# Two transformer blocks on one core: attention maps handled two heads at a time, and work regrouped around the norms

## The chip, the cores and the metric

The kernel runs on one core of a Trainium2 chip. The metric is the device time of one execution, in microseconds. The engines are TensorE (PE, with PEld its weight load), VectorE (DVE), ScalarE (ACT), GpSimd (POOL) and SyncE (SP), which issues most transfers.

## The reference, cut to what matters

256 tokens of width 1024 pass through two blocks in float32. Shortened:

```python
h = layer_norm(x)
y = hybrid_mixer(h)       # 4 forgetting heads (64), 4 differential heads (two maps of 32 each),
                          # 4 gated recurrent heads (128) with decays exp(cumsum(log_f))
h = layer_norm(ALPHA * h + y)
h = layer_norm(ALPHA * h + memory_attention(h, mem))    # 4 heads of 256
h = layer_norm(ALPHA * h + grouped_moe(h))              # 16 experts, 2 per token
# second block, layer 0
h = norm(ALPHA_2 * h + even_mixer(h))     # 8 latent heads with top-64 keys, 8 window heads with sinks
h = norm(ALPHA_2 * h + cross_attention(h, mem))         # 4 heads of 128
h = norm(ALPHA_2 * h + dense_swiglu(h))
# second block, layer 1
h = norm(ALPHA_2 * h + odd_mixer(h))      # 16 heads, three branches: compressed, selected, window
h = norm(ALPHA_2 * h + cross_attention(h, mem))
h = norm(ALPHA_2 * h + moe_swiglu(h))                   # 8 experts, 2 per token
# one attention map
p = softmax(q @ k.T * scale + bias_and_mask)            # 256 queries x 256 keys
o = p @ v
```

## The kernel before, in words

Every engine has its own hand-written instruction stream; semaphores order them. The stages follow one another in each stream.

**Units and chunks.** A projection is a list of `units` (lines 515 to 612). For each, PE fills PSUM bank `B[2 + u % 2]` (`emit`, L1017) and ACT copies it out (`save_unit`, L1624). A weight chunk (1 MB, a slot of `ring`) is split into a high half by ACT (`weight_highs`, L1600, instruction at L1607) and a low half by DVE (`weight_lows`, L1959, instruction at L1965); PE makes three products per tile (L997 to L999). There are two slots for high halves, so two chunks can be ready ahead. A chunk freed by PE lets ACT and then DVE prepare the next one but one.

**Output projections.** `add` on PE (L1145) makes four column blocks; DVE adds each to `h` and takes its statistics (L2043, L1954). The high half that follows the last block (`feed`, L1831) and its low half (`lows_through_adds`) stand ahead of the norm. `layer_norm` (L1999) asks ACT for a square root (`root`, L1596), scales `h` in two halves (L2017), and PE transposes each (L1068), ACT saving it to `hT` (L1631).

**Attention.** A map is one head's 256 by 256 softmax. Its steps, map by map: PE `logits` (L1160) into `F[m % 2]`; DVE `score_map` (L2051): add the mask into `S` (L2063), take the maximum (L2070); ACT `exps` (L1673), which also sums; DVE `normalise` (L2078): reciprocal (L2082), a gate (L2084), two scalings (L2086); PE `transpose_probs` (L1176) into `F[2 + m % 2]`; ACT `save_probs` (L1683) to `PT` (L1687); PE `values` (L1187); ACT `save_group` (L1689). PE runs `logits(i)`, `transpose_probs(i - 2)`, `values(i - 3)` in turn (L1211). There are three `S` buffers and two `PT` buffers. Stages: `mix1` (4 forgetting, 8 differential maps), `mem1` (4), `mix2` (8 window, 8 latent), `xa0` (4), `mix3` (32), `xa1` (4). In a two-pass float32 matmul the trace has two records per instruction.

**Recurrent heads.** After all of `mix1` is projected, DVE and ACT turn the forget logits into log decays (L2382 to L2397 and L1841 to L1849); PE, DVE, ACT and POOL then work in 8 levels (`hgrn`, L1219; arguments L2413, exponentials L1855, operands on POOL L933, masks L2428). Three mean squares (`sumsq`, L1654 and L1656) follow.

**Bias tiles.** A relative bias of a head is one flip matmul (L1085) of rows that POOL loads (`hankel_rows`, L920): 16 tiles before `mix2`, 8 more (heads 8 to 15) before `mix3`, whose load POOL issues when norm 6 has been scaled (L923). The compressed logits of `mix3` are one small matmul per head and token half (L1555).

**What the change leaves alone.** The two routed layers (`moe1`, `moe2`) and the steps of the dense layer.

Of the kernel before, what the change touches and what calls it, by code (L numbers as in the profile page):

```python
# [29 lines left out]
P = 128  # L30
T = 256
# [138 lines left out]
def two_block_kernel(nc, I, out):  # L170
    ctx = ExitStack()
    with ctx:
# [23 lines left out]
        NS = 3  # L196
        S, S_r = sb_rounded("S", [P, NS, TT, T])
# [51 lines left out]
        Wlv = r.get(2, 4, T)  # L249
        SM = r.get(3, 512)  # L250
# [46 lines left out]
        olatT = qlatT  # L297
        idx_act = r.get(2, TT, T)
# [13 lines left out]
        vc4 = r.get(2, 64)  # L312
        assert r.at <= 15872 - 16 * BIAS_W, r.at
# [58 lines left out]
        logits_ready, scored, max_ready = sem("logits_ready"), sem("scored"), sem("max_ready")  # L372
# [147 lines left out]
        project("mix1", "T", hT, w, dqT, 772, 1, scale=32.0 ** -0.5)  # L520
        project("mix1", "T", hT, w, dkT, 1028, 1)
        project("mix1", "tok", hT, w, dv, 1284, 1)
        project("mix1", "tok", hT, w, hi, 2564, 2)
        project("mix1", "T", hT, w, hqT, 1540, 2, func=ACT.Silu)
        project("mix1", "T", hT, w, hgT, 3076, 2, func=ACT.Silu)
        unit("forget sums", "cum", (nlogf, FOX_H), cumq, ACT.Copy, -1.0)
        unit("mean squares", "sumsq", (halves, dsq, 1.0 / 64), drs)
# [18 lines left out]
        for i in range(2):  # L546
            for j in range(8 * i, 16):
                unit(f"bias tiles {i}", "flip", (j,), biasT[:, j, :])
# [22 lines left out]
            else:  # L571
# [18 lines left out]
                for par in range(2):  # L590
                    adds.append(("compressed logits", None, par, None))
                for par in range(2):
                    unit("compressed probs", "pctr", (par,), pcT[:, par])
                residual("out3", I["od_w_out_2"][0])
            transposes(f"ln{3 * i + 4} transposed", h, hT, 3 * i + 4)
            project(f"xa{i} queries", "T", hT, I["xa_w_q_2"][i], mqT, 0, 2, scale=128.0 ** -0.5)
            residual(f"xa{i} out", I["xa_w_o_2"][i], 4)
            transposes(f"ln{3 * i + 5} transposed", h, hT, 3 * i + 5)
            if i == 0:
                experts("dense", FF_DENSE // COLS)  # L600
            else:
# [7 lines left out]
        maps, groups, map_span = [], [], {}  # L609

        def attention(stage, items):
# [10 lines left out]
            map_span[stage] = (m0, len(maps), g0, len(groups))  # L622

# [7 lines left out]
        def diff_map(j, c):  # L631
            rows = slice(32 * (2 * (j % 2) + c), 32 * (2 * (j % 2) + c) + 32)
            return dict(qk=[(dqT[rows, j // 2, :], dkT[rows, j // 2, :])], mask=chunkmask,
                        coef=neglam if c else None, v=dv[:, :, 64 * j:64 * j + 64], base=64 * (j % 2))
        diff = [([diff_map(j, c) for j in (2 * a, 2 * a + 1) for c in range(2)], yT[:, 2 + a, :]) for a in range(2)]
# [18 lines left out]
        def nsa_maps(j):  # L654
            g = j // 8
            out = []
            for branch, (k, v) in enumerate(((ksT, vs), (kwT, vw))):
                out.append(dict(qk=[(qcT[half(j), j // 2, :], k[half(j), g, :])], mask=bias_of(j),
                                coef=g3[:, :, 3 * j + 1 + branch], v=v[:, :, 64 * g:64 * g + 64], base=64 * (j % 2),
                                compressed=j if branch == 0 else None))  # L660
            return out
        attention("mix3", [(nsa_maps(2 * a) + nsa_maps(2 * a + 1), yT[:, a, :]) for a in range(8)])
# [206 lines left out]
        def _(pool):  # L869
# [72 lines left out]
            for n in range(4, 6):  # L942
                load_gb(n)
# [13 lines left out]
            load_gb(6)  # L957
            pool.wait_ge(normed_half, 14)
            hankel_rows(list(range(8, 16)), 0)
            for n in range(7, 10):  # L960
# [20 lines left out]
        def _(pe):  # L981
# [12 lines left out]
            def product(bank, x_hi_, x_lo_, w_hi_, w_lo_, start, stop):  # L994

                x1, x2, w1, w2 = (v.bitcast(R32) for v in (x_hi_, x_lo_, w_hi_, w_lo_))
                mm(bank, x1, w1, start=start, stop=False)  # L997
                mm(bank, x1, w2, start=False, stop=False)  # L998
                return mm(bank, x2, w1, start=False, stop=stop)  # L999
# [17 lines left out]
            def emit(u):  # L1017
                stage, kind, args, dest, _, _ = units[u]
                x_hi_, x_lo_ = halves_mem if kind in ("T", "tok") and args[0] is memT else halves_hT
                of = {"mem1 values": "mem1 keys", "mix2b": "mix2"}.get(stage, stage)  # L1020
# [1569 lines left out]
```

## Time and profile before

| | us |
|---|---|
| runs | 2647.33, 2657.49, 2663.75 (median 2657.49) |
| the profiled execution | 2651.68 |
| its span | 2649.9 |
| PE busy | 2356.4 (89%) |
| DVE busy | 1630.2 (62%) |
| ACT busy | 1265.9 (48%) |
| POOL busy | 106.2 (4%) |
| mean granted PE clock | 0.924 |

Times in the views are counted from the span's start. Around the span lie 1.8 us that belong to the measured time. Where the stages lie: start and `mix1` projections to 161 us, gates to 178, `mix1` attention to 229, recurrent levels to 277, `out1` to 322, `mem1` to 402, `moe1` 436 to 696, memory keys and bias tiles to 786, `mix2` to 950, `xa0` to 1003, dense layer 1020 to 1211, `mix3` projections 1239 to 1341, its attention to 1455, `out3`, `xa1` to 1532, `moe2` 1556 to 2632.

### The profile page before, as it was taken

Reading aid. Unit: us, or ns where it says so; the run is one execution under the profiler, and the core shown is the slowest. Engines: PE = TensorE matmul, PEld = TensorE weight load, DVE = VectorE, ACT = ScalarE, POOL = GpSimd, SP = SyncE. Lnnn points to the kernel's source line nnn. Section 1 sums busy time; section 2 is a strip of 40 time slices with the busy share of each in tenths; the row PEclk is TensorE's granted clock in tenths of the full one; section 3 lists DMA queues with packets and bytes.
Section 4 is the critical chain, followed back from the end, with each engine's and each line's share of the span. In section 5 each row is a group of like instructions: output and inputs, shape, how many; then the busy total and the mean of one; then the engine's idle time right before and its main releaser. Section 6 shows DMA issues by size and latency. Waiting matters only on the chain.

```text
span 2649.9 us, 31609 instructions
## 1 busy us (share of the span) xinstructions
PE 2356.4 (89%) x12540; PEld 1846.6 (70%) x12540; DVE 1630.2 (62%) x1835; ACT 1265.9 (48%) x1372; POOL 106.2 (4%) x89
## 2 busy tenths in 40 slices
PE   8977697999889887997889869999999999999995
PEld 7965686333568577996755757777778777878774
DVE  4436453111435656775057668878888888888885
ACT  4343342111233534443225347767676767666662
POOL 3002000000000001221000000000000000000000
PEclk9979897999888898998959879999999999999997
DMA  8430125999643024554600249989999999989892
GB/s 272 153 96 1 64 80 192 417 413 416 228 126 125 17 80 160 182 181 151 147 0 1 80 170 361 343 316 343 336 347 328 340 336 328 357 309 361 314 359 108
DMA packets 285683, 592.17 MB, mean 223 GB/s; under 512 B 12123, under 2 KB 118015, under 8 KB 277248
## 3 DMA queue, kind: packets, MB, share of 16 engines
q1 hardware_dynamic: 280000, 571.54, 60.9%
q0 software_dynamic: 5568, 19.06, 2.3%
q8 instruction: 76, 1.25, 0.2%
q14 instruction: 39, 0.32, 0.0%
HBM read 589.45 MB, written 1.11 MB: 223 GB/s over the span
## 4 chain that ended last, share of the span: by engine, by line
PE 74%; DMA 10%; ACT 6%; DVE 6%; issue 3%; POOL 0%; SPq 0%; DVEq 0%; ACTq 0%
PE psF L997 9%; PE psF L999 9%; PE psF L998 9%; PE psB L997 8%; PE psB L998 8%; PE psB L999 8%; DMA ring<-in_moe_w_gate_dram 4%; DMA ring<-in_w_dram 4%; PE psF L1169 3%; PE psB L1204 3%; PE psF L1331 2%; PE psB L1353 2%; ACT arena_rounded L1753 2%; PE psB L1052 1%; PE psF L1182 1%
## 5 line engine op out<-in xcount | busy, mean ns | idle before, releaser
L2252 DVE TENSOR_TENSOR ring_rounded<-ring,arena_rounded 128x2048 fp32r<-128x2048 f32 x224 | 507.0, 2287 | 29.5 <-ACT arena_rounded L1753 29.2
L1753 ACT ACTIVATE arena_rounded<-ring 128x2048 fp32r<-128x2048 f32 x224 | 429.5, 1919 | 196.2 <-DMA ring<-in_moe_w_up_dram 135.3
L997 PE MATMUL psF<-arena_rounded 128*128 128x512 f32 x896 | 360.4, 402 | 3.4 <-ACT arena_rounded L1775 1.5
L999 PE MATMUL psF<-arena_rounded 128*128 128x512 f32 x896 | 355.6, 397 | 0.0
L998 PE MATMUL psF<-ring_rounded,arena_rounded 128*128 128x512 f32 x896 | 354.6, 396 | 0.0
L1965 DVE TENSOR_TENSOR ring_rounded<-ring,ring_rounded 128x2048 fp32r<-128x2048 f32 (+1 forms) x71 | 153.9, 2171 | 191.4 <-ACT ring_rounded L1607 191.3
L997 PEld LDWEIGHTS psF<-arena_rounded 128*128 128x128 f32 x896 | 170.2, 190 | 44.2 <-issue 4.9
L999 PEld LDWEIGHTS psF<-arena_rounded 128*128 128x128 f32 x896 | 169.6, 189 | 39.7
L998 PEld LDWEIGHTS psF<-ring_rounded,arena_rounded 128*128 128x128 f32 x896 | 169.8, 190 | 37.7
L1607 ACT ACTIVATE ring_rounded<-ring 128x2048 fp32r<-128x2048 f32 (+1 forms) x71 | 128.5, 1812 | 118.0 <-PE psF L999 80.7
L998 PE MATMUL psB<-ring_rounded,PT_rounded 128*128 128x512 f32 x448 | 178.2, 398 | 0.0
L2252 DVE TENSOR_TENSOR ring_rounded<-ring,memT_rounded 128x2048 fp32r<-128x2048 f32 x56 | 128.4, 2292 | 45.8 <-ACT memT_rounded L1753 45.8
L2252 DVE TENSOR_TENSOR ring_rounded<-ring,mv_rounded 128x2048 fp32r<-128x2048 f32 x56 | 128.4, 2292 | 32.8 <-ACT mv_rounded L1753 32.8
L997 PE MATMUL psB<-yT_rounded,ring_rounded 128*128 128x256 f32 x464 | 137.7, 297 | 5.8 <-ACT hT L1631 5.6
L1753 ACT ACTIVATE memT_rounded<-ring 128x2048 fp32r<-128x2048 f32 x56 | 107.4, 1918 | 69.4 <-DMA ring<-in_moe_w_down_dram 69.4
L1331 PE MATMUL psF<-ring,arena 128*64 128x512 f32 x512 | 119.1, 609 | 21.9 <-DMA ring<-in_w_dram 21.0
L998 PE MATMUL psB<-memT_rounded,ring_rounded 128*128 128x256 f32 x464 | 136.3, 294 | 0.0
L999 PE MATMUL psB<-yT_rounded,ring_rounded 128*128 128x256 f32 x464 | 136.1, 293 | 0.0
L1753 ACT ACTIVATE mv_rounded<-ring 128x2048 fp32r<-128x2048 f32 x56 | 107.4, 1918 | 57.4 <-DMA ring<-in_moe_w_down_dram 57.4
L1680 ACT ACTIVATE S<-S,small 128x256 f32<-128x256 f32 x144 | 71.9, 499 | 98.8 <-DVE small L2070 98.8
L997 PE MATMUL psB<-memT_rounded,PT_rounded 128*128 128x512 f32 x224 | 93.3, 416 | 15.1 <-DVE PT_rounded L2257 15.1
L997 PE MATMUL psF<-ring_rounded,hT_rounded 128*128 128x256 f32 x320 | 93.5, 292 | 13.0 <-DVE memT_rounded L1988 10.4
(384 smaller groups left out, 4870.8 us busy)
## 6 DMA issues: line engine op xcount, KB each, us to landing
ring<-in_moe_w_gate_dram SPq DMA_DIRECT2D x112, 1024.0 KB, 5.2
ring<-in_moe_w_up_dram SPq DMA_DIRECT2D x112, 1024.0 KB, 5.1
ring<-in_moe_w_down_dram SPq DMA_DIRECT2D x112, 1024.0 KB, 4.9
ring<-in_w_dram SPq DMA_DIRECT2D x96, 1024.0 KB, 8.9
ring<-in_w_in_dram SPq DMA_DIRECT2D x14, 1024.0 KB, 5.4
ring<-in_ff_w_gate_dram SPq DMA_DIRECT2D x11, 1024.0 KB, 7.3
ring<-in_ff_w_up_dram SPq DMA_DIRECT2D x11, 1024.0 KB, 9.7
ring<-in_ff_w_down_dram SPq DMA_DIRECT2D x11, 1024.0 KB, 5.0
```

The source lines that it names most:

```text
L997: mm(bank, x1, w1, start=start, stop=False)
L998: mm(bank, x1, w2, start=False, stop=False)
L999: return mm(bank, x2, w1, start=False, stop=stop)
L1169: last = mm(bank[:, T * t:T * t + T], q[:, P * t:P * t + P], k, start=(i == 0), stop=(i == n - 1))
L1204: last = mm(bank[base:base + w, 2 * piece:2 * piece + T], mp["v"][:, k, piece:piece + w], PT[:, m % 2, k, :], start=(first and k == 0), st ...
L1331: ins = mm(bank[rows(g), :], xgT[:, kk, rows(g)], ws[g][0][:, k, :], start=first_, stop=last_)
L1353: ins = mm(Y[c][rows(g), :], hiddenT[:, ff, rows(g)], ws[g][0][:, f, cols], start=first_, stop=last_)
L1607: ap_(ring_r[:, hi_slot[c], 0:kt * w].bitcast(R32), ring[:, slot_of[c], 0:kt * w], ACT.Copy)\
L1680: ins = ap_(S[:, s, t], S[:, s, t], ACT.Exp, bias=nmx[:, s, t:t + 1], accum_out=ssum[:, s, t:t + 1])
L1753: ap_(w_hi[slot].bitcast(R32), ring[:, slot], ACT.Copy).then_inc(q["high"], 1)
L1965: V.tensor_tensor(ring_r[:, slot_of[c], 0:kt * w].bitcast(R32), raw, ring_r[:, hi_slot[c], 0:kt * w], ALU.subtract).then_inc(weights_low, 1)
L2252: V.tensor_tensor(ring_r[:, slot].bitcast(R32), ring[:, slot], w_hi[slot], ALU.subtract)\
```

## The change

- Attention works on bundles: two maps where heads are 64 wide, else one. The matmuls of the two maps alternate in `logits` and `values`; the reciprocal, the gate and the sink steps serve both maps at once. Logits use all four `F` banks, transposes `B[2]` and `B[3]`. In `mix1`, `mix2` and `mix3` there are six `S` and four `PT` buffers, in arena memory that is free then. Map order in `mix1` and `mix3` is changed so that neighbours belong to different heads.
- Adding the mask and taking the maximum becomes one DVE instruction per token half, `tensor_tensor_reduce`. Forgetting maps keep the two old steps. Maps without a mask (`mem1`, `xa0`, `xa1`) are no longer copied: the maximum and the exponential read PSUM.
- The gate chain goes inside the first units of `mix1` (after the queries, keys and values of the forgetting heads), with the first two level arguments. The later arguments are made one level earlier. The differential squares are made at level 2, the other squares in two halves, and `out1` does its first four row blocks for two column blocks early.
- Behind `out1`, `out2`, `out3` the last high and low halves are made after the square root and after the transposed inputs. Before the dense layer, the two first chunks' halves are spread around the norm.
- Bias tiles 8 to 15 of the second set are made at norms 4 and 5; their rows are loaded after the attention of `mix2`. Norm 6 is followed by the transposes. The ring starts at slot 3 after the dense layer.
- Compressed logits: a pair of heads shares one matmul over 128 rows, `kcT` being block diagonal: 16 matmuls where there were 32.

Cut to its core:

```diff
-        NS = 3
+        NS = 6
...
+            bundles[stage], m = [], m0
+            while m < len(maps):
+                two = maps[m]["v"].shape[2] == 64
+                bundles[stage].append((m, m + 1) if two else (m,))
+                m += 2 if two else 1
...
-            def logits(m):
-                mp, bank = maps[m], F[m % 2]
-                if m >= 2:
-                    pe.wait_ge(scored, m - 1)
+            def logits(bundle):
+                for m in bundle:
+                    if maps[m]["at"] >= 4:
+                        pe.wait_ge(max_ready if "mask" in maps[m] else exp_ready, m - 3)
...
+                    for i in range(n):
+                        for m in bundle:
+                            mp, bank = maps[m], F[maps[m]["at"] % 4]
...
+                            last = mm(bank[:, T * t:T * t + T], q, k, start=(i == 0), stop=(i == n - 1))
...
+                    for k in range(TT):
+                        for m in bundle:
...
+                            last = mm(B[mp["group"] % 2][mp["base"]:mp["base"] + w, 2 * piece:2 * piece + T],
+                                      mp["v"][:, k, piece:piece + w], pt_of(m)[:, k, :],
...
             def attend(stage):
...
+                    if i < len(todo):
+                        logits(todo[i])
+                    if 0 <= i - 2 < len(todo):
+                        for m in todo[i - 2]:
+                            transpose_probs(m)
+                    if 0 <= i - 3:
+                        values(todo[i - 3])
...
-                    ins = V.tensor_tensor(S[:, s], bank, mp["mask"], ALU.add)
...
-                ins = V.tensor_reduce(nmx[:, s], S[:, s], AX.X, ALU.max, negate=True)
+                        for t in range(TT):
+                            ins = V.tensor_tensor_reduce(out=buf[:, t], in0=bank[:, t], in1=more[:, t], scale=-1.0,
+                                                         scalar=-TAKEN, op0=ALU.add, op1=ALU.min,
+                                                         accum_out=nmx[:, n, t:t + 1])
...
+                do(V.reciprocal(scales, sums_))
+                if mp.get("coef") is not None:
+                    do(V.tensor_tensor(scales, scales, mp["coef"], ALU.mult))
...
# ScalarE, inside the projections
+            forget = span("mix1")[0] + 3
+            for u in range(*span("mix1")):
+                save_one(u)
+                if u == forget:
+                    request()
+                    answer(ap_(lame, lams, ACT.Exp))
+                    request()
+                    step.did(ap_(ffe, ffa, ACT.Exp, scale=-1.0))
+                    step.wait()
+                    request()
+                    step.did(ap_(hkT, bcT, ACT.Exp, scale=-1.0))
+                    step.wait()
+                elif u == forget + 1:
+                    answer(ap_(ffe, ffe, ACT.Ln, bias=1.0))
+                    step.did(ap_(bcT, hkT, ACT.Ln, bias=1.0))
+                    step.wait()
+                elif u == forget + 2:
+                    answer(ap_(hkT, hfT, ACT.Sigmoid, scale=-1.0))
...
# ScalarE, recurrent levels
+            for lv in range(2, len(LEVELS)):
+                level_decay(lv)
+                if lv == 2:
+                    save("differential squares")
             for a in range(2):
-                ins = ap_(oT[:, 2 * a:2 * a + 2, :], pair(B[a]), ACT.Copy)
-            answer(ins)
+                act.wait_ge(hg_pv, 2 * len(LEVELS) + a)
+                answer(ap_(oT[:, 2 * a:2 * a + 2, :], pair(B[a]), ACT.Copy))
             save("mean squares")
             feed("out1")
             root()
+            feed_last("out1")
...
# VectorE, recurrent levels
-                if lv + 1 < len(LEVELS):
-                    level_argument(lv + 1)
+                if 3 <= lv + 2 < len(LEVELS):
+                    level_argument(lv + 2)
...
# TensorE
-            add("out1")
+            add("out1", early=4)
...
+                        for jj in range(8):
+                            last = mm(F[a % 4][:, 32 * jj:32 * jj + 32], qcT[:, jj, P * t:P * t + P], kcT[:, jj // 4, :],
+                                      start=True, stop=True)
...
# GpSimd
+            load_gb(4)
+            pool.wait_ge(o_saved, groups_end("mix2"))
+            hankel_rows(list(range(8, 16)), 0)
+            load_gb(5)
...
-            pool.wait_ge(normed_half, 14)
-            hankel_rows(list(range(8, 16)), 0)
```

## Rows read from the trace of the kernel before

**Rows 1.** Windows: stretch: us, then busy us (instructions) of each engine, granted clock, DMA.

```profile
161.00:178.00 17.00, 2.38 (x14) 2.08 (x12) 6.19 (x9) 12.57 (x13) 0.00 (x0) 0.67 0.19 62
178.00:229.00 51.00, 49.94 (x176) 28.50 (x176) 27.66 (x71) 21.09 (x64) 0.00 (x0) 0.81 0.00 0
229.00:277.00 48.00, 34.86 (x273) 33.34 (x272) 27.56 (x36) 8.84 (x9) 21.24 (x16) 0.89 0.00 1
277.00:298.00 21.00, 7.25 (x21) 3.77 (x19) 6.78 (x9) 12.73 (x14) 0.00 (x0) 0.72 0.00 0
...
865.00:924.00 59.00, 49.02 (x196) 30.26 (x198) 43.07 (x108) 32.50 (x103) 0.00 (x0) 0.86 0.00 1
...
1341.00:1382.00 41.00, 39.37 (x96) 21.37 (x97) 21.16 (x51) 13.80 (x45) 0.00 (x0) 0.50 0.00 0
1382.00:1455.00 73.00, 72.28 (x322) 40.08 (x320) 54.98 (x148) 39.38 (x124) 0.00 (x0) 1.00 0.00 1
1560.00:2649.00 1089.00, 1026.49 (x4488) 821.32 (x4488) 880.67 (x568) 721.56 (x497) 0.00 (x0) 0.97 0.90 321
```

**Rows 2.** Timeline of ACT at the start and in the gate chain.

```profile
68.40 0.20 ACT L1833 ACTIVATE small<-small 128x2 f32<-128x2 f32 x1 [1.52 <-DVE small L2371]
...
163.93 1.28 ACT L1841 ACT_TABLE_LOAD   x1
...
174.33 1.06 ACT L1849 ACTIVATE arena<-arena 128x1024 f32<-128x1024 f32 x1
```

**Rows 3.** Groups of PE, 1383 to 1448 us (`mix3`): xcount | busy us, mean ns.

```profile
L1169 PE MATMUL psF<-arena 64*128 64x256 f32 x88 | 24.8, 402 | 0.0
L1204 PE MATMUL psB<-PT,arena 128*64 128x256 f32 x88 | 23.7, 392 | 0.0
L1182 PE MATMUL psF<-cw,S 128*128 128x128 f32 x91 | 15.0, 286 | 0.0
L1197 PE MATMUL psB<-arena 15*64 15x256 f32 x23 | 7.5, 401 | 0.0
```

**Rows 4.** Groups of DVE, 1383 to 1448 us.

```profile
L2063 DVE TENSOR_TENSOR S<-psF,arena 128x512 f32<-128x512 f32 x23 | 15.9, 691 | 12.3 <-PE psF L1169 12.3
L2070 DVE TENSOR_REDUCE small<-S 128x2 f32<-128x512 f32 x22 | 15.1, 686 | 0.7
L2086 DVE TENSOR_SCALAR S<-S,small 128x256 f32<-128x256 f32 x44 | 13.6, 351 | 0.8
L2084 DVE TENSOR_TENSOR small<-small,g 128x2 f32<-128x2 f32 x22 | 3.6, 161 | 0.8
```

**Rows 5.** Groups of ACT, 1383 to 1448 us.

```profile
L1680 ACT ACTIVATE S<-S,small 128x256 f32<-128x256 f32 x44 | 22.0, 500 | 30.3 <-DVE small L2070 30.3
L1687 ACT ACTIVATE PT<-psF 128x512 f32<-128x512 f32 x22 | 12.6, 574 | 0.0
```

**Rows 6.** Timeline of PE: first logits of two window heads; the `uv` unit.

```profile
865.93 1.14 PE L1169 MATMUL psF<-arena 64*128 64x256 f32 x8 [0.59 <-ACT arena L1642]
...
923.86 2.22 PE L1107 MATMUL psB<-arena,wuv 128*64 128x256 f32 x16 [0.47 <-ACT arena L1694]
```

**Rows 7.** Timeline of DVE: a `tensor_tensor_reduce` and its read-out, `mix2`.

```profile
814.97 0.28 DVE L2464 CUSTOM_DVE_ANT_0 arena<-arena 128x128 f32<-128x128 f32 x1
815.17 0.08 DVE L2464 DVE_READ_ACCUMULATOR2_ANT small<- 128x1 f32 x1
```

**Rows 8.** Timeline of DVE at norm 1.

```profile
324.19 2.29 DVE L1965 TENSOR_TENSOR ring_rounded<-ring,ring_rounded 128x2048 fp32r<-128x2048 f32 x1 [0.59 <-ACT ring_rounded L1607]
326.39 0.38 DVE L2009 BATCH_NORM_AGGREGATE small<-small 128x2 f32<-128x24 f32 x2
```

**Rows 9.** Timeline, norm 6: rows loaded, then the bias tiles.

```profile
1217.27 0.91 POOL L923 DMA_DIRECT2D arena<-bias_rows  x1 [16.70 <-DVE h L2017]
...
1225.84 8.46 PE L1085 MATMUL psB<-arena,cw 128*128 128x384 f32 x16 [15.36 <-issue]
```

**Rows 10.** Timeline of PE: the compressed logits.

```profile
1320.18 13.01 PE L1555 MATMUL psF<-arena 64*128 64x15 f32 x64 [0.40 <-ACT arena L1670]
```

More of the change, by code:

```diff
@@ L546, in two_block_kernel @@
         for i in range(2):
-            for j in range(8 * i, 16):
-                unit(f"bias tiles {i}", "flip", (j,), biasT[:, j, :])
+            if i == 0:
+                for j in range(16):
+                    unit("bias tiles", "flip", (j,), biasT[:, j, :])
             transposes(f"ln{3 * i + 3} transposed", h, hT, 3 * i + 3)
@@ L594, in two_block_kernel @@
                 residual("out3", I["od_w_out_2"][0])
+            if i == 0:
+                for j in range(8, 12):
+                    unit("bias tiles again", "flip", (j,), biasT[:, j, :])
             transposes(f"ln{3 * i + 4} transposed", h, hT, 3 * i + 4)
@@ L597, in two_block_kernel @@
             residual(f"xa{i} out", I["xa_w_o_2"][i], 4)
+            if i == 0:
+                for j in range(12, 16):
+                    unit("last bias tiles", "flip", (j,), biasT[:, j, :])
             transposes(f"ln{3 * i + 5} transposed", h, hT, 3 * i + 5)
@@ L605, in two_block_kernel @@
                 routed("moe2")
-        maps, groups, map_span = [], [], {}
+        more_s = {stage: Region(at).get(3, TT, T) for stage, at in more_at.items()}
+        more_pt = {stage: Region(0 if stage == "mix2" else at + 3 * TT * T).get(2, TT, T) for stage, at in more_at.items()}
+        maps, groups, map_span, bundles = [], [], {}, {}
         def attention(stage, items):
@@ L1019, in emit @@
                 x_hi_, x_lo_ = halves_mem if kind in ("T", "tok") and args[0] is memT else halves_hT
-                of = {"mem1 values": "mem1 keys", "mix2b": "mix2"}.get(stage, stage)
+                of = {"mem1 values": "mem1 keys", "mix1b": "mix1", "mix2b": "mix2"}.get(stage, stage)
                 bank = B[2 + u % 2]
@@ L1568, in _ @@
                 add(f"xa{i} out")
+                if i == 0:
+                    run("last bias tiles")
                 run(f"ln{3 * i + 5} transposed")
@@ L1906, in _ @@
                 feed(f"out{i + 2}")
+                if i == 0:
+                    tiles = span("bias tiles again")[0]
+                    for u in (tiles, tiles + 1):
+                        save_one(u)
                 root()
+                if i == 0:
+                    for u in (tiles + 2, tiles + 3):
+                        save_one(u)
+                feed_last(f"out{i + 2}")
                 save(f"ln{3 * i + 4} transposed")
@@ L1912, in _ @@
                 if i == 0:
-                    for part in range(2):
-                        dense_high(0, 0, part)
+                    tiles = span("last bias tiles")[0]
+                    for u in (tiles, tiles + 1):
+                        save_one(u)
                 root()
+                if i == 0:
+                    for u in (tiles + 2, tiles + 3):
+                        save_one(u)
+                    dense_high(0, 0, 0)
                 save(f"ln{3 * i + 5} transposed")
```

500 lines of the change are left out of this document (278 added, 222 removed).

## The prediction, made before the changed kernel ran

> **What bounds the kernel now.** I read the chain of waits first, then the busy shares in windows by stage, then groups and timelines of the stages that the change touches. The chain shows `moe1` (260 us), the dense steps (190 us) and `moe2` (1076 us) as stretches of their own, whose inner steps stay; the last of them is PE-bound, 1026.49 of 1089 us busy [rows 1]. So the change can move only what lies between. There the windows show four kinds of time:
>
> - gates: 17 us in which PE is busy 2.38 and ACT 12.57 [rows 1]. Each function begins with a table load of 1.28 us, and full-size functions take 1.06 [rows 2];
> - attention: PE is busy throughout, 72.28 of 73 us in the second part of `mix3`, and also 39.37 of 41 us in its first part, but there at a granted clock of 0.50, the lower of its two levels (1.2 against 2.4 GHz). 96 records in 41 us against 322 in 73 us: 0.43 against 0.227 us a record [rows 1];
> - recurrent levels: PE 34.86 of 48 us, POOL 21.24 [rows 1];
> - squares: 21 us with PE 7.25 and ACT 12.73 busy [rows 1].
>
> All sums are against the profiled execution, 2651.7 us (span 2649.9 and 1.8 around it); the median of the runs is 5.8 above it.
>
> **1. Start.** ACT loads a table (1.28), idles 1.52 for DVE and computes 0.20 before it saves the bias rows, and PE waits for that [rows 2]. The change moves this behind: 2.9 us.
>
> **2. Gates, 11 us.** The chain of 17 us goes. What stays behind the last projection is ACT's save (0.6) and high half (1.9), then the cumulative sum: 3 us. So 14 are saved. The chain now lies inside units of 5.8 us each (85 us of `mix1` for 14 chunks). ACT has 2.5 us of work in such a unit, so 3.3 are free, but the order is in line: two loads, two exponentials and a wait for DVE come to 5. The halves for the next but one chunk have only about 1 us to spare, so I expect one stall of 1 us, and 2 more where DVE's scans and level arguments (2.4 and 2.8 us) stand ahead of a low half. Bounds: 0 and 8 us (every piece of the chain uncovered beyond its unit). I take 3, the nearer to the counted slack.
>
> A page bears on it: the Trainium skill, "ScalarE: Activation LUTs", under what ACT_TABLE_LOAD costs, says some 2.7 us, and that one table set holds both ln and exp. The rows show 1.28 us, and the trace has a load at every turn between the two. By the page's price the five loads that are moved would cost 7 us more in place of the 1 us stall; the measured duration decides.
>
> **3. Attention, by pairs.** One map of `mix3` at full clock costs PE four records of each kind: logits 24.8/88 x 4 = 1.13, values 1.08, transposes 0.66, and for every second map 0.65 of compressed values [rows 3]; 2.92 with overlaps. Do two alternating matmuls run side by side? The trace before has both cases. The first two window heads lie on rows 0 to 63 and 64 to 127: their 8 records take 1.14 us, what 4 take in steady state. Two 64-column halves alternate in `uv`: 16 records in 2.22 us, 0.14 each against 0.27 [rows 6, 3]. So a pair costs PE 1.13 + 1.08 + 1.1 (transposes don't pair) + 0.33 = 3.6 us, less overlaps 3.4.
>
> DVE for a pair: the mask step and the maximum, 0.69 each per map [rows 4], become two fused instructions. The trace has them at 128 elements only, 0.28 us with a read-out of 0.08 mostly under the next [rows 7]; with the slope between this and 0.69 at 512 I get 0.42, with read-out 0.45. Bounds at 256 elements: 0.31 (the scaling) and 0.69 (the full-width step), a spread of -0.6 to +1.0 us a pair. Pair: 4 x 0.45 + 4 x 0.31 + two small ops 0.36 with gaps + 0.1 = 3.5 us. ACT: 4 x 0.5 + 2 x 0.57 [rows 5] + 0.2 = 3.3. The three engines are close, so I take a step of 3.65 us, bound by DVE, where two maps took 5.84.
>
> A pair in the low-clock stretch is bound by PE: 3.4 x 1.9 = 6.4.
>
> The Trainium skill, "TensorEngine Tiling (Array Packing)", under the PSUM bottleneck, warns that tiling speeds TensorE and not the evacuation. By PE alone the step would be 3.4; by the warning it is DVE's. The rows agree with the warning, and what more it could cost is the second rival.
>
> *`mix3`*: before 113 us (1341 to 1455). How long the lower clock lasts is open: after an idle stretch it stayed 17 us in `mix2`, 31 from the gates on, 41 here. I take 30: fill 5, four pairs at 6.4, twelve at 3.65, inputs for `out3` 2.5 of 4.5 us, drain 5: 82. With 17 us it would be 74, with 41 us 87. Gain 31 (26 to 39).
> *`mix1`*: before 51, its first 20 us at the low clock because PE had idled for the gates. Now PE comes warm. Forgetting pairs: 4.6 us of logits each (the cumulative part is 128 rows and doesn't pair), then five steps at 3.5 to 4.7 and a drain of 5: 32. Gain 19 (10 if the clock falls all the same).
> *`mix2`*: 59 before. Four window pairs, three of them still slow at 5.8, and eight single maps at 2.75 where they took 3.1 (the fused step; PE then binds): 48. Gain 10.
> *`mem1`, `xa0`, `xa1`*: one copy of 0.69 less ahead of each maximum: 0.7 + 1.7 + 1.7 = 4.
>
> **4. Recurrent levels, 9 us.** Two levels' operands exist at the start (before, PE waited 7 us). Then each level needs 3.85 us of PE, against 4.8 before, since an argument no longer stands behind the masks. Against this stands the differential square at level 2: its two table loads and functions, 12.7/3 = 3.9 us less the copies [rows 1], delay level 3 by 3.8. 48 becomes 38. DVE's share of a level is 3.7 to 3.8 us under POOL's use of memory, so the bound could flip: 4.0 a level, a gain of 8.
>
> **5. Squares and `out1`, 16 us.** From the last level to the end of `out1` it was 45 us. Now two squares of 3.9 follow one another on ACT (8.4 us after the level), then 2.7 of DVE: pair 3 comes at 11. Meanwhile PE makes 48 of the 192 products (6 us). The other 144 take 17, and the third and fourth weight halves are late by 1.3: 11 + 17 + 1 = 29.
>
> **6. Norms 1, 4, 7: 8 us.** Between the statistics and the aggregate stand the high and the low half, 2.29 us and the wait ahead of it; 2.85 us go [rows 8]. They come later, with 5.8 us of cover in the first unit. At norm 4 ACT saves two tiles and a high half ahead of the transposed blocks, 0.5 late. 2.85 + 2.3 + 2.85. The rows of the bias are loaded after `mix2`; before, they needed 8.6 us (1217.27 to 1225.84) [rows 9], and 24 us of `out2` cover that.
>
> **7. Norm 5, 3 us.** The second high and low half (a landing at 1005.2, then 1.9 and 2.3) leave the path: 5 us earlier, but DVE's tail of the norm then meets POOL's low half and holds the first dense step: 3.
>
> **8. Norm 6, 15 us.** PE waited until 1225.84 for the rows and spent 8.46 us on eight tiles [rows 9]. Products began at 1238.7. Without them they start when ACT, after its two high halves (1214.8 to 1218.7), has saved the four transposed pairs: 1223.2.
>
> **9. Compressed logits, 6.5 us.** 64 records of 0.203 us [rows 10], set by the weight load and not by the 15 columns; 32 remain.
>
> Sum: 2.9 + 11 + (31 + 19 + 10 + 4) + 9 + 16 + 8 + 3 + 15 + 6.5 = 135. 2651.7 - 135 = 2516.7; with the median 5.8 above the profiled execution, 2522 us.
>
> **The rivals.**
> *Alternating matmuls don't overlap* in the long run (10 records of mode changes instead): PE stays at 2.92 a map, which gives back 28 us in `mix3`, 7 in `mix1`, 5 in `mix2`: 2562. Against it speak [rows 6]. 5%.
> *Hand-offs bind*: in-order waits between three engines at 90% load make the step 4.5, and the fused instruction is at its upper bound: 26 pairs x 0.85 = 22 us: 2544. For it: the engines are nearly even. 22%.
> *The lower clock stays through attention*, as PE is less busy: 12 pairs of `mix3` at 6.4 in place of 3.65 add 33, `mix1` adds 9: 2564. Against it: in `mix2`, 49.02 of 59 us busy, it rose after 17 us. 7%.
> *Slower than before*: the lower clock also holds in the projections that follow those stages. They hold about 390 us of products at full clock, twice that at the lower. From 135/390 = 35% of them on, the gain is gone; at 45% the time is 2522 + 175 = 2697. Nothing shows the clock low in a dense run of products beyond 17 us. 2%.
> *No effect*, the moved work landing on another queue in full: 2650. 2%.
> *My forecast*: 62%, of which a quarter is a clock that rises early, 2508.
>
> **Range.** The forecast's own terms give 2495 to 2545 (the low clock 17 to 41 us in `mix3`, the fused step's bounds, the stalls in the gates 0 to 8). With the first three rivals: 2488 to 2574.
>
> Faster by over 1%: 0.96; within 1% (about what a measurement of this kernel can tell from no change): 0.02; slower by over 1%: 0.02.
>
> **What would show it.** Logits of a pair as 8 records in 1.15 us; values likewise; in `mix3` at full clock 3.65 us a pair with DVE above 90% busy; no PE gap of 14 us before the cumulative sum, at most 3 us of gaps in `mix1`'s projections; 3.85 us a level from level 4 on; 29 us from the last level to the end of `out1`; first product 8 us after norm 6's square root; compressed logits in 6.5 us. Wrong would be a PE still contiguous in `mix3` at over 5 us a pair, a fused instruction above 0.6 us, or `moe2` longer than 1076 us.

## The result and the profile after

| | before | after |
|---|---|---|
| median | 2652.41 (4 runs) | 2498.85 (4 runs: 2491.49 to 2503.91) |
| profiled execution | 2651.68 | 2497.97 |
| its span | 2649.9 | 2496.2 |
| mean granted clock | 0.924 | 0.947 |

The ratio of the times (after over before) is 0.9424, with a 95% interval of 0.9365 to 0.9483: faster by 154 us. The forecast was 2522 (2488 to 2574). Direction and range held; the gain was 19 us larger than the 135 of the sum.

Windows of the kernel after, by stage. The columns are the stretch and its us, the busy us (instructions) of PE, PEld, DVE, ACT and POOL, the granted clock, then the DMA share and GB/s. They answer to [rows 1]: the wait for the gates, the attention of `mix1`, the recurrent levels, squares with `out1`, the attention of `mix2`, that of `mix3`, and `moe2`.

```profile
163.00:166.00 3.00, 1.28 (x13) 1.19 (x11) 0.04 (x1) 2.46 (x3) 0.00 (x0) 1.00 0.45 152
166.00:199.00 33.00, 27.05 (x176) 17.69 (x176) 23.00 (x79) 22.91 (x67) 4.95 (x4) 1.00 0.05 19
199.00:241.00 42.00, 34.50 (x275) 32.83 (x276) 28.23 (x34) 11.11 (x13) 18.46 (x12) 0.96 0.00 1
241.00:271.00 30.00, 25.57 (x196) 23.73 (x196) 17.44 (x22) 14.93 (x13) 0.00 (x0) 1.00 0.33 106
810.00:855.00 45.00, 36.19 (x196) 25.08 (x194) 31.01 (x128) 30.61 (x101) 0.07 (x1) 0.89 0.00 1
1245.00:1308.00 63.00, 57.51 (x416) 35.48 (x416) 50.13 (x231) 50.55 (x168) 0.00 (x0) 0.96 0.00 1
1406.00:2496.00 1090.00, 1026.05 (x4493) 820.61 (x4491) 882.31 (x569) 722.96 (x498) 0.00 (x0) 0.97 0.90 321
```

The instruction counts of PE are about those of before (416 records in the attention of `mix3`, 418 then); the stages are shorter. How long the clock was low in a window follows from its column: with the two levels 1.00 and 0.50 it is 2 x (1 - clock) x length. For `mix3` that is 63 x 0.08 = 5 us, where [rows 1] have 41 us in one piece. `moe2` has not changed.

Timeline of PE in the same stage, two pairs of maps: start, us, engine, line, operation, tiles, instructions; in brackets the idle time before and what ended it.

```profile
1272.23 1.13 PE L1232 MATMUL psF<-arena 64*128 64x256 f32 x8
1273.29 1.10 PE L1242 MATMUL psB<-cw,S 128*128 128x128 f32 x8
1274.32 1.08 PE L1266 MATMUL psB<-arena 128*64 128x256 f32 x8
1275.34 1.14 PE L1232 MATMUL psF<-arena 64*128 64x256 f32 x8
1276.91 0.63 PE L1242 MATMUL psB<-cw,S 128*128 128x128 f32 x4 [0.43 <-ACT PT L1777]
1277.39 0.63 PE L1242 MATMUL psB<-cw,arena 128*128 128x128 f32 x4
1277.94 0.65 PE L1256 MATMUL psB<-arena 15*64 15x256 f32 x4
1278.52 1.08 PE L1266 MATMUL psB<-PT,arena 128*64 128x256 f32 x8
1279.54 1.13 PE L1232 MATMUL psF<-arena 64*128 64x256 f32 x8
```

Eight records of logits take 1.13 us and eight of values 1.08, what four of each took in [rows 3]. From logits to logits it is 3.11 us for the pair without the compressed branch and 4.20 with it: 3.655 on average, the 3.65 of the prediction. The groups of VectorE from 1256 to 1300 us (xcount | busy us, mean ns) show the fused step:

```profile
L2200 DVE CUSTOM_DVE_ANT_0 S<-psF,arena 128x256 f32<-128x256 f32 x24 | 8.9, 421 | 4.9 <-PE psF L1232 4.9
L2224 DVE TENSOR_SCALAR S<-S,small 128x256 f32<-128x256 f32 x24 | 7.0, 349 | 0.3
L2200 DVE DVE_READ_ACCUMULATOR2_ANT small<- 128x1 f32 x47 | 3.9, 83 | 0.0
```

One lasts 0.42 us, as taken. Its read-out is hidden, though, and the next begins before its end: four in a row start 0.35 us apart, where I had 0.45.

Stage by stage, gains from the timelines of PE in both kernels:

| step | forecast | measured |
|---|---|---|
| 1 start | 2.9 | 0.8 |
| 2 gates | 11 | 11.1 |
| 3 attention of `mix3` | 31 | 50.3 (113.2 to 62.9) |
| `mix1` | 19 | 18.4 (51.1 to 32.6) |
| `mix2` | 10 | 12.8 (57.4 to 44.7) |
| `mem1`, `xa0`, `xa1` | 4 | 5.6 |
| 4 levels | 9 | 6.4 (48.2 to 41.8) |
| 5 squares, `out1` | 16 | 15.0 |
| 6 norms 1, 4, 7 | 8 | 7.3 |
| 7 norm 5 | 3 | 4.2 |
| 8 norm 6 | 15 | 16.2 |
| 9 compressed logits | 6.5 | 6.0 |
| all else | 0 | -0.4 |

The last row hides shifts of up to 2.3 us in both directions in stages whose instructions are the same; a term under 2 us is not to be read more closely. Steps 1 and 5 to 8, some 43 us, are read from the two timelines alone; no run below varies them by themselves.

### The profile page after: what moved, and what is told of

Its sections match the earlier page's. It is cut to its first block, busy times and chain, and to the rows that moved or that the text cites. A ratio compares the mean times of both kernels' runs of the same rounds, so it can differ in the third digit from the quotient of the medians.

```text
span 2496.2 us, 31567 instructions
## 1 busy us (share of the span) xinstructions
PE 2250.2 (90%) x12508; PEld 1791.1 (72%) x12508; DVE 1580.0 (63%) x1887; ACT 1255.6 (50%) x1370; POOL 109.0 (4%) x89
## 4 chain that ended last, share of the span: by engine, by line
PE 71%; DMA 11%; ACT 8%; DVE 7%; issue 2%; SPq 0%; POOL 0%; DVEq 0%; ACTq 0%; POOLq 0%
PE psF L1039 9%; PE psF L1041 9%; PE psF L1040 9%; PE psB L1039 8%; PE psB L1040 8%; PE psB L1041 8%; DMA ring<-in_w_dram 4%; DMA ring<-in_moe_w_gate_dram 4%; PE psF L1399 2%; PE psB L1421 2%; ACT arena_rounded L1848 2%; PE psB L1094 2%; PE psB L1266 1%; ACT ring_rounded L1680 1%; PE psF L1232 1%
## 5 line engine op out<-in xcount | busy, mean ns | idle before, releaser
L1399 PEld LDWEIGHTS psF<-ring,arena 128*64 128x64 f32 x512 | 40.4, 141 | 92.3 <-issue 92.3
L1041 PE MATMUL psB<-mv_rounded,PT_rounded 128*128 128x512 f32 x264 | 104.2, 395 | 0.0
```

Of the source, the lines that this page charges most:

```text
L1041: return mm(bank, x2, w1, start=False, stop=stop, skip_group_check=open_groups)
L1399: ins = mm(bank[rows(g), :], xgT[:, kk, rows(g)], ws[g][0][:, k, :], start=first_, stop=last_)
```

## Experiments

Each starts from the kernel after unless said otherwise. Effects of under 1% are read from stages of the profile.

**Maps of a pair one after the other.** Is it the alternation that makes matmuls overlap?

```diff
-                for piece in range(0, width, P):
-                        for m in bundle:
+                for m in bundle:
+                    for piece in range(0, width, P):
```

and the same in `logits`.

> The changed kernel, but with the two maps of a pair computed one after the other by TensorE (logits and values), all else kept: buffers, fused maximum, order of the stages. Theory (alternating matmuls on the two halves of the array run side by side): a pair of mix3 then needs 2.2 of logits, 2.1 of values, 1.1 of transposes and 0.33 of compressed values, 5.7 us in place of 3.65, so the attention of mix3 grows from 63 us by at least 33, that of mix1 from 33 by about 12, that of mix2 by about 4: some 50 us in all. Rival (the deeper buffers and the shorter VectorE work made the gain, the order of the matmuls nothing): the step stays below 4.2 us and the time within 12 us. On the clock, which stayed low for 6 us of mix3's attention where it had been 41: if the denser pairs bring it back, it is low for 20 us and more here and mix3's attention takes 105 us or more; if the shorter stage ahead of the attention does, it is low for about 6 us again and the attention takes 96 to 99.

Measured: 2515.5 us, ratio 0.9468 (0.9427 to 0.9509). Windows over the attention of `mix1` and of `mix3`:

```profile
164.00:214.00 50.00, 48.10 (x175) 28.36 (x175) 22.84 (x79) 22.60 (x66) 4.94 (x4) 0.60 0.03 11
1260.00:1323.00 63.00, 57.69 (x416) 36.76 (x416) 50.54 (x231) 50.59 (x168) 0.00 (x0) 0.95 0.00 1
```

The logits of a pair in the timeline of PE, in `mix3`:

```profile
1287.66 1.14 PE L1232 MATMUL psF<-arena 64*128 64x256 f32 x8
```

In `mix3` nothing changed: 63.1 us, and the eight records still take 1.14 us, though in the program both matmuls of the one map now stand before those of the other. So my theory was wrong about alternation, and the stated rival did not hold either, as the records do overlap. In `mix1` the stage took 50.8 us. There each map of a forgetting head has full-height matmuls of its cumulative part behind its half-height one, so that taking the maps in turn parts the two halves; and the clock was low for 40 of 50 us. That the one led to the other is argued, not shown. The next run separates the two properties.

**Full-width work between the halves.**

```diff
-                    if i < len(todo):
-                        logits(todo[i])
+                    for p in range(2):
+                        if i < len(todo):
+                            logits(todo[i][p:p + 1])
```

and so for `transpose_probs` and `values`: one map's three steps, then the other's.

> The changed kernel, but TensorE takes the pair map by map: logits, transposes and values of the first map, then those of the second, so that the full-width transposes stand between the matmuls of the two halves of the array. Buffers, VectorE and ScalarE are as in the change. The run before showed that inside a pair the order of the matmuls does not matter. Theory (matmuls of different halves run side by side when nothing of full width stands between them): here they don't, a pair costs TensorE 5.7 us in place of 3.65, mix3's attention goes from 63 to 97 us or more, the whole time up by some 45. Rival (the overlap was never what shortened the stage; deeper buffers and a lighter VectorE were): mix3's attention stays under 68 us. On the clock: if the pairs bring it back, it stays low here for 20 us and more of mix3's attention; if not, for 3 to 9 us as in the four profiles of the change so far.

Measured: 2565.8 us, ratio 0.9679 (0.9644 to 0.9713). The same two windows:

```profile
166.00:225.00 59.00, 57.28 (x176) 31.84 (x176) 23.57 (x79) 23.92 (x69) 4.94 (x4) 0.68 0.04 12
1279.00:1386.00 107.00, 105.39 (x416) 58.88 (x416) 51.36 (x231) 53.06 (x168) 0.00 (x0) 0.85 0.00 1
```

One map of `mix3` in the timeline of PE:

```profile
1329.67 1.13 PE L1234 MATMUL psF<-arena 64*128 64x256 f32 x4
1330.73 0.66 PE L1244 MATMUL psB<-cw,S 128*128 128x128 f32 x4
1331.32 1.08 PE L1270 MATMUL psB<-arena 128*64 128x256 f32 x4
```

Four records need the 1.13 us of eight again; two maps take 3.22 + 2.65 = 5.87 us where they took 3.65. `mix3`'s attention is back at 106.8 us, with 32 us of it at the lower clock. (The profile is of this kernel's slowest execution, 2581.3 us.) With everything else of the change in place, this order alone gives back 67 us (0.9679 - 0.9424 of 2652): the neighbourhood of the two halves carries 44% of the gain (by the two intervals, 67 us give or take some 18), and buffers and fused steps without it shorten `mix3` by only 6 us.

**The kernel before, once more, and with filled gaps.** First unchanged:

> The kernel before, unchanged, for a second profile. If the 40 us of lower clock in mix3's attention and the 19 us in mix1's belong to its instructions, they come again within 7 us; if they are chance, they differ by more, as the 0 and 13.7 us of lower clock did that two profiles of the same instructions of the changed kernel show in mix1's attention.

Then with unread matmuls of 128x128 on 512 columns in its waits:

```diff
+            filler(14)
             pe.wait_ge(logf_ready, 1)
...
+                    filler(4)
                     pe.wait_ge(proj_saved, saved("compress parts"))
...
+                    filler(5)
                     pe.wait_ge(cmp_ready, 1)
```

> The kernel before with such matmuls in its three waits: 14 in the 14 us ahead of the cumulative sum, 4 and 5 ahead of mix3's attention. If the gaps were why the clock was low in the attention stages (19 and 29 us of mix1's, 40 and 40 us of mix3's in two profiles), it is now low for less than 10 us of each, mix1's attention takes 41 to 43 us and mix3's 94 to 98. If the unpaired matmuls themselves keep it low, mix3's attention still has 25 us and more at the lower clock and takes 106 or more.

Windows of the unchanged kernel's second profile (attention of `mix1`, of `mix3`):

```profile
180.00:236.00 56.00, 54.59 (x176) 30.82 (x176) 27.91 (x71) 21.54 (x66) 0.00 (x0) 0.74 0.00 0
1347.00:1460.00 113.00, 111.44 (x416) 61.29 (x416) 75.65 (x199) 52.53 (x167) 0.00 (x0) 0.82 0.00 1
```

Windows with fillers: the filled gap, `mix1`, the end of the fillers ahead of `mix3`, `mix3`:

```profile
164.00:178.00 14.00, 11.56 (x31) 5.64 (x29) 5.90 (x9) 10.27 (x12) 0.00 (x0) 0.94 0.17 58
178.00:233.00 55.00, 53.97 (x176) 30.60 (x176) 27.94 (x71) 21.20 (x65) 0.00 (x0) 0.74 0.00 0
1337.00:1341.00 4.00, 3.27 (x15) 1.73 (x13) 3.96 (x7) 1.08 (x2) 0.00 (x0) 1.00 0.00 0
1341.00:1454.00 113.00, 110.86 (x416) 60.53 (x416) 75.66 (x199) 52.78 (x168) 0.00 (x0) 0.83 0.00 1
```

And `mix3`'s attention with fillers in two parts:

```profile
1341.00:1381.00 40.00, 38.47 (x96) 20.40 (x97) 20.68 (x51) 13.50 (x44) 0.00 (x0) 0.53 0.00 0
1382.00:1454.00 72.00, 71.39 (x318) 39.53 (x316) 54.83 (x148) 39.28 (x124) 0.00 (x0) 1.00 0.00 1
```

The 41 us in `mix3` came again to the microsecond; in `mix1` it was 29 where it had been 19, outside the 7 us that I had allowed. With the gaps filled the clock was at its upper level when `mix3`'s attention began (1.00) and nearly throughout the gap ahead of `mix1` (0.94), and yet 38 us of the one stage and 29 of the other ran at the lower. So the gaps were not the cause: in `mix3` the clock fell 2.6 us after the unpaired attention had begun, and stayed low while PE was busy for 38.47 of 40 us. Being unpaired is not the whole of it either. In all three profiles of these instructions the clock rose with some 73 us of the same unpaired work left, and stayed up to the end (1.00 over the last 72 us here, and over 73 us in [rows 1]). What brings it back, no run shows.

**Sixty-four compressed logits, as before.**

```diff
-                        for jj in range(8):
-                            last = mm(F[a % 4][:, 32 * jj:32 * jj + 32], qcT[:, jj, P * t:P * t + P], kcT[:, jj // 4, :],
+                        for t in range(TT):
+                            for jj in range(8):
+                                last = mm(F[a % 4][:, o:o + N_CMP], qcT[half(j), j // 2, P * t:P * t + P],
```

> The changed kernel with the compressed logits as before: 64 matmuls of 15 columns in place of 32. The stage grows by 6.0 to 6.5 us. On the clock: if the shorter stage ahead of mix3's attention is why the clock came back 6 us into it, it now stays low for 20 us and more of it and mix3's attention grows by another 7 us or more; if the pairs bring it back, the attention stays at 63 to 66 us.

One run, 2510.7 us. The logits took 13.01 us against 7.04, 6.0 more; `mix3`'s attention stayed at 62.8 us (clock 0.97). The shorter stage ahead is not what brought the clock back. `mix1`, whose instructions are those of the change, took 36.7 us, with 14 at the lower clock.

**Gate chain behind the projections.** The blocks of ScalarE and VectorE that ran after units 3 to 5 of `mix1` stand behind `mix1b`.

> The changed kernel with the gate chain behind the last projection of mix1. TensorE idles 13 to 15 us ahead of the cumulative sum again and the two stalls of 0.7 and 1.7 us in the projections go: 11 us more. On the clock: it falls in this gap. If pairs bring it back, it is low for less than 10 us of the attention, which grows from 33 to at most 38; if the clock goes by its own time after a gap, it stays low for most of the attention, as in the kernel before (19 us), and the attention takes 42 or more.

One run, 2515.5 us. From the first transposes to the attention it took 7.7 us more, not 11: PE waited 9.6 us, not 14. (The changed chain lets the cumulative sum go as soon as its own operand is there; that this is the difference is argued, not tried.) The clock fell in the gap and was back 6 us into the attention, then was low for 14 more: 39.5 us in all, between the two expectations.

**Fused step undone.**

```diff
-                        for t in range(TT):
-                            ins = V.tensor_tensor_reduce(...)
+                        do(V.tensor_tensor(buf, bank, more, ALU.add))
+                        ins = V.tensor_reduce(nmx[:, n], buf, AX.X, ALU.max, negate=True)
```

> The changed kernel with the fused addition-and-minimum undone: one full-width addition and one full-width maximum per map. Theory (TensorE sets the 3.65 us step by now and VectorE has 0.5 us of slack): VectorE's work per pair grows from 3.2 by 1.4 to 4.6, so the step becomes 4.6 and mix3's attention grows by about 14 us, mix2's by 4, mix1's by 2: 20 in all. Rival (TensorE's own work covers it): step up to 3.9, under 6 us in all.

Measured: 2528.9 us, ratio 0.9541 (0.9505 to 0.9576); `mix3` 74.7 us, `mix2` 51.3, `mix1` 39.1.

```profile
1259.00:1333.00 74.00, 59.23 (x416) 36.37 (x414) 68.16 (x167) 52.69 (x167) 0.00 (x0) 0.92 0.00 1
```

VectorE is busy 92% now and PE 80%. Steps alternate 3.52 and 4.76 us, 4.14 on average where no halves for `out3` are made; I had expected 4.6. The fused step is worth some 30 us once the halves overlap, again give or take 18; 25 of them lie in `mix1`, `mix2` and `mix3` of the profile.

**Compressed values left out, and four maps of scores.** Which engine sets the step, and do the buffers matter?

```diff
-                    if mp.get("compressed") is not None:
-                        mm(B[g % 2][mp["base"]:mp["base"] + 64, 0:T], vc4[rows, j // 8, :], pcT[rows, j % 2, j // 8, :],
```

> The changed kernel without the compressed branch's values: the 15-row matmuls of every second pair are left out, so the compressed branch is missing from the output. Theory (TensorE sets the step by its own work, 3.55 of 3.65 us): the long step of 4.21 us shortens by 0.65 to about 3.6, the mean to 3.35, mix3's attention from 63 to 58. Rival (VectorE, ScalarE and the hand-offs between the three set it): the mean step stays above 3.55 and the attention above 61.5 us.

```diff
-        NS = 6
+        NS = 4
```

> The changed kernel with room for 4 maps of scores in place of 6. Theory (the depth carries a part of the gain): VectorE may score a pair only when TensorE has transposed the pair before last, which it does after the new logits, so a loop of scoring 1.4, normalising 1.5 and transposing 1.1 us closes at 4.2 us a pair with its waits; mix3's attention goes from 63 to about 72. Rival (the 6 buffers are slack): it stays within 2 us.

Windows over `mix3`'s attention, without the compressed values and with four maps:

```profile
1246.00:1306.00 60.00, 53.10 (x384) 34.05 (x384) 50.10 (x231) 50.35 (x168) 0.00 (x0) 0.95 0.01 1
```

```profile
1253.00:1327.00 74.00, 60.60 (x416) 37.03 (x416) 50.48 (x231) 50.81 (x167) 0.00 (x0) 0.92 0.00 1
```

Without 0.65 us of PE work in every second pair the long step fell from 4.20 to 3.53 or 3.63 us, the average to 3.37, and the attention to 59.8 us. PE's own work set the step, but closely: two later steps, behind VectorE's halves for `out3`, took 3.90 and 3.89 us with waits of 0.71 us for ScalarE, and the stage came out between the 58 of the theory and the 61.5 of the rival. With four maps the steps are 3.71 and 4.87 (4.29; 4.2 expected) and the attention takes 74.4 us: the depth is part of the gain. Each of these two is one run (2497.1 and 2518.1 us) and read by its stage.

**Differential squares later.**

```diff
-                    if lv == 2:
+                    if lv == 5:
                         pe.wait_ge(squares_ready, 1)
...
-                if lv == 2:
-                    save("differential squares")
+            save("differential squares")
...
-                if lv == 4:
+                if lv == 7:
```

Three stalls of PE in the levels of the kernel after led there. Timeline of PE (after):

```profile
204.94 1.16 PE L1295 MATMUL psB<-arena 128*128 128x128 f32 x8 [1.29 <-DVE arena L2581]
...
213.21 1.01 PE L1318 MATMUL psF<-arena 128*128 128x128 f32 x3 [2.68 <-POOL arena L976]
...
223.75 0.94 PE L1295 MATMUL psB<-arena 128*128 128x128 f32 x6 [2.63 <-DVE arena L2581]
```

ScalarE shows the second one's cause, the table load and function ahead of level 3's exponentials:

```profile
207.70 1.28 ACT L1736 ACT_TABLE_LOAD   x1
208.99 0.63 ACT L1736 ACTIVATE arena<-arena 128x512 f32<-128x512 f32 x1
209.53 1.99 ACT L1955 ACTIVATE arena<-arena 128x1024 f32<-128x1024 f32 x2
```

> The changed kernel with the differential squares later: TensorE computes them at level 5, ScalarE takes their two functions behind all levels' exponentials, VectorE their product and halves at level 7. Theory (of the 41.8 us of the recurrent levels, 2.7 are ScalarE's table loads ahead of level 3's exponential and 2.6 VectorE's product and halves ahead of level 4's masks, at a time when all three engines still prepare levels): the first stall goes in full, the second becomes under 1 us, since VectorE idles 1.1 us in each half level at the end; the levels take 37 to 38 us, the time falls by 4. Rival (the levels' own chain over VectorE, ScalarE and GpSimd is late anyway): they stay above 40 us.

Measured: 2493.6 us, ratio 0.9386 (0.9348 to 0.9424). The levels took 35.9 us in place of 41.8, with stalls of 1.29, 0.72 and 0.32 us left. As a time it is not told from the change (the intervals overlap); as a stage it is 6 us.

**Fillers ahead of `mix3`,** with the `filler(4)` and `filler(5)` shown above, and then in every longer wait.

> The changed kernel with matmuls that nobody reads, 128x128 on 512 columns, in two waits of TensorE ahead of mix3's attention: 4 in the 4.2 us after the hidden parts and 5 in the 5.5 us of the compressed softmax. Theory A (idleness of TensorE lets the clock fall there): the 27 us of lower clock from 20 us ahead of the attention on don't come or are shorter than 10; compressed logits and probabilities get 2 to 3 us faster, the attention falls from 63 to 58 or 59. Theory B (it is the thin matmuls, of few rows or columns, that lower it, and full ones alone hold it): the clock comes back by the filler, ahead of the attention, but falls again; 2 to 4 us in all. Rival (the fillers at the lower clock take 1.7 us each and end late): the time rises by 3 to 6 us.

One run, 2499.2 us. The stretch from the hidden parts to the attention took 37.5 us in place of 40.7. Windows from 1224 on: the fillers and small steps, the compressed logits and second fillers, the first pairs:

```profile
1224.00:1234.00 10.00, 8.86 (x73) 5.68 (x68) 0.00 (x0) 7.61 (x11) 0.00 (x0) 0.97 0.81 267
1234.00:1244.00 10.00, 10.00 (x28) 6.54 (x28) 5.40 (x14) 0.60 (x1) 0.00 (x0) 0.51 0.00 0
1244.00:1257.00 13.00, 8.58 (x60) 5.78 (x58) 12.60 (x48) 8.83 (x31) 0.00 (x0) 1.00 0.00 0
```

The clock stays up to 1233, past the first fillers; it falls 1.3 us into the compressed logits and stays low through most of the second fillers, though PE has not a free microsecond in these 10. It went as theory B said (3 us), but which property of the small matmuls counts was not varied.

> The changed kernel with the late differential squares (6 us of the recurrent levels in the run above) and with unread full matmuls in the waits of TensorE at the norms, ahead of the dense step, ahead of mix3's attention and ahead of moe2: 2 to 5 of 0.85 us in waits of 2 to 6 us. If the clock falls at the norms because TensorE waits there, the stretches of lower clock of 7 to 14 us at norms 4 to 8, and the 27 and 10 us ahead of moe2, shrink to less than half in sum; with 3 us of the stage ahead of mix3 that gives 2499 - 6 - 3 - 10 = 2480 us. If the fillers only end late, at 1.7 us each at the lower clock, the time is that of the late squares alone, 2493, or above. Under the ratio 0.9386 of the late squares alone would be a gain by the fillers.

Measured: 2489.2 us, ratio 0.9383 (0.9356 to 0.9410). Against 0.9386 for the late squares alone the fillers bring nothing that can be told, although the mean granted clock rose (0.953 to 0.959 in the five executions, 0.942 to 0.947 with the late squares alone). The first product of `moe2` came at 1407.0 us, 7 us earlier than in the profile of the late squares alone (1414.2), but `moe2` itself took 3 us more; and ahead of the dense layer five fillers took 7.5 us, as they ran at the lower clock themselves. It is the lowest median of the study, but its interval overlaps that of the change.

## Why the prediction was right, and where its sizes were off

**The part on which the sum rested held.** Halves that overlap, a step of 3.65 us, gates inside the projections (stalls 0.7 + 1.7 us, 3 taken), weight halves behind norms (2.76 us at norms 1 and 7, 2.85 forecast), norm 6, the compressed logits: within 1.3 us each.

On the table loads the rows of before decided, and rightly, but I set them against only half of what the page says. The Trainium skill, "ScalarE: Activation LUTs", section "What ACT_TABLE_LOAD costs", makes up its 2.7 us of a load of about 1.28 us and a drain of about 1.38 us. This trace agrees on the load; of the drain it shows nothing: the load at 207.70 us begins 0.02 us after the function before it ends.

**Step 3, `mix3`: 82 us forecast, 62.9 measured; this is the error of 19.** Two terms were mis-sized. "I take 30" for the lower clock gave four pairs at 6.4 in place of 3.65 us, 11 us; it was low for 5 us only. And fill 5, inputs for `out3` 2.5 and drain 5 counted 12.5 us beside the 16 pairs: 62.9 - 16 x 3.655 = 4.4 was left, as logits of the first pairs and values of the last overlap with other pairs, and the halves lie in VectorE's slack.

Behind the first stands a wrong reading. I took the clock as something that an idle stretch before the stage lowers, and that then takes its time to return. The trace of before already showed the lower level with PE busy ahead of the attention, in the compressed logits; I had not laid this stretch beside the forecast:

```profile
1320.00:1333.00 13.00, 12.82 (x64) 12.82 (x64) 0.41 (x1) 1.42 (x2) 0.00 (x0) 0.50 0.01 1
```

Filled gaps in the kernel before left it low for 38 us of `mix3` and 29 of `mix1`; the change with its halves set apart, 32 of `mix3`; the change and the variants that keep its halves adjoining there, 0 to 13 us. So the lower clock goes with unpaired halves in `mix3`, but not with all of their work. Nor does PE's busy share order them: 105.39 of 107 us busy went with a clock of 0.85, 59.23 of 74 with 0.92. My third rival (the lower clock stays, "as PE is less busy") had this the wrong way round. The Trainium skill, "TensorE: Matmul & The Clock Gate", section "What's actually happening", says that the gate follows how busy PE has been recently; in this case a PE busy throughout ran at the lower level for tens of us, so that rule does not suffice here. Which property of unpaired half-array matmuls counts stays open, and so does why the clock rose again 41 us into the same work: their shape and their kind were not varied by themselves. By [rows 1] (0.43 against 0.227 us a record, 96 records) the low stretch cost the kernel before about 19 of the 113 us of `mix3`, an estimate.

**The step's bound was named wrongly, its size not.** I said "bound by DVE", above 90% busy. The window shows otherwise:

```profile
1253.00:1304.00 51.00, 46.27 (x352) 28.23 (x348) 42.67 (x200) 44.15 (x146) 1.00 0.01 1
```

PE 91%, ACT 87%, DVE 84%. The fused instructions follow one another at 0.35, not 0.45 us, so DVE needs about 3.1 us a pair and not 3.5. PE's own work is the 3.4 us of the prediction, and a wait of 0.43 us for ScalarE in every second pair, 0.2 on average, makes up the rest of 3.65. The run without compressed values shows the bound; the run with two steps shows how near DVE is. The warning that I weighed there, that of the Trainium skill, "TensorEngine Tiling (Array Packing)", section "PSUM Bottleneck", that tiling speeds TensorE and not the evacuation, did not decide in this trace: emptying PSUM left those 0.2 us of waits.

**Hand-offs (second rival, 22%)** did not come about at six maps: 3.65, not 4.5. With four maps they do: 4.29.

**Step 4, the levels: 38 forecast, 41.8 measured.** "3.85 a level" was too much: undisturbed levels go at 3.57 (a half level every 1.79 us from 228 on), set by PE. "Delay level 3 by 3.8" fitted the stall of 2.68. What I left out is VectorE's product and halves at level 4 (0.74 + 0.43 + 0.69 us ahead of the masks, a stall of PE of 2.63 us), and a stall of 1.29 us behind the level arguments ahead of level 1's masks. The late squares took most of the stalls of 2.68 and 2.63 us away.

**Step 1: 2.9 forecast, 0.8 measured.** The bias rows' wait went (4.25 to 1.23 us), but PE came to this point 2.5 us later, behind other work of the first stage whose instructions are unchanged.

**`mix1`: 32 forecast, 32.6 measured, and partly luck.** In this profile the clock never fell in it. In five others with the same instructions (64 compressed logits, late squares, both kernels with fillers, no compressed values) it took 36.2 to 36.8 us, with 10 to 14 us at the lower level. A fair forecast for the stage would have been 36.

## What to carry to other kernels

Where a head fills only half of TensorE's rows or columns, let the matmuls of two heads on different halves adjoin in the program, with nothing of full width between; their order inside the group is free. Judge such a change by the chain of all engines: here buffers and fused VectorE step shortened `mix3` by 6 us without the overlap, and undoing either of them with it cost 12 (62.9 to 74.7 and to 74.4 us). Don't carry a stage's clock over as if it belonged to the gap before it; look whether the same instructions bring it each time, and take two profiles of a kernel before a term of 10 us rests on it.

## What had not been expected of the hardware

- Two matmuls of one half, then two of the other, overlap as well as alternating ones: eight records in 1.14 us either way. The Trainium skill, "TensorEngine Tiling (Array Packing)", section "Key Properties", says that tiles operate independently; this trace agrees, and shows that it takes no alternation.
- TensorE's clock stayed at its lower level while PE had next to no idle time: 41 us in `mix3` in both profiles of the kernel before, 12.82 us busy of 13 at 0.50 in its compressed logits, and 10 of 10 at 0.51 in compressed logits and fillers of a variant. It rose again within unchanged work.
- One profile is one sample: the same instructions of `mix1`'s attention of before had 19 and 29 us at the lower clock, those of the change 0 to 14.
- A fused add-and-minimum over 256 columns starts every 0.35 us, though each lasts 0.42.
